# Down weights of the expert loop loaded through ScalarE's DMA queue, up weights through SyncE's

## What is computed

```python
def moe(h, w_router, b_router, w_gu, b_gu, w_down, b_down):
    logits = (xt @ w_router + b_router).astype(jnp.float32)
    top_v, top_i = lax.top_k(logits, TOP_K)          # 4 of 32 experts per token
    gates = jax.nn.softmax(top_v, axis=-1)
    ...
    gu = xblk @ w_gu[e] + b_gu[e]                    # 1024 x 2048 per expert
    gate = jnp.minimum(gu[:, :D_EXPERT], SWIGLU_LIMIT)
    up = jnp.clip(gu[:, D_EXPERT:], -SWIGLU_LIMIT, SWIGLU_LIMIT)
    act = (up + 1.0) * (gate * jax.nn.sigmoid(SWIGLU_ALPHA * gate))
    return act @ w_down[e] + b_down[e]               # 1024 x 1024 per expert
```

## Time and profile before

| | us |
|---|---|
| median of 3 runs | 1126.22 (1125.59 to 1127.43) |
| the profiled execution, its time | 1125.18 |
| its span in the profile | 1123.40 |
| PE busy | 1091.3 (97% of the span) |
| VectorE busy | 246.7 (22%) |
| ACT busy | 108.8 (10%) |
| GpSimd (POOL) busy | 28.7 (3%) |
| HBM read | 433.66 MB, 387 GB/s over the span |

### The profile page before, as it was taken

The page is one execution under the profiler, slowest core; times in us unless marked ns, Lnnn a source line. Parts: engine busy times, 40 slices in busy tenths (PEclk is TensorE's granted clock), DMA queues, the critical chain, the costliest instruction groups (busy, mean ns, idle before and its releaser), DMA issues.

```text
span 1123.4 us, 12562 instructions
## 1 busy us (share of the span) xinstructions
PE 1091.3 (97%) x5328; PEld 486.5 (43%) x5329; DVE 246.7 (22%) x580; ACT 108.8 (10%) x245; POOL 28.7 (3%) x43
## 2 busy tenths in 40 slices
PE   8999999999999999999999999999999999999996
PEld 6758887734333333333333333333333333333322
DVE  3263212332121212121212221111121212121121
ACT  1152120300000000000000000000000000000001
POOL 1240000000000000000000000000000000000000
PEclk9999999999999999999999999999999999999998
DMA  9964386489999999999999999999999999999996
GB/s 355 407 239 167 113 294 244 184 348 422 418 419 438 431 433 431 429 429 431 433 436 431 434 431 429 429 431 435 435 431 433 431 429 429 432 426 428 423 420 258
DMA packets 31149, 435.14 MB, mean 387 GB/s; under 512 B 4560, under 2 KB 5328, under 8 KB 8720
## 3 DMA queue, kind: packets, MB, share of 16 engines
q1 hardware_dynamic: 30272, 432.76, 91.7%
q10 hardware_dynamic: 848, 1.97, 0.5%
HBM read 433.66 MB, written 1.05 MB: 387 GB/s over the span
## 4 chain that ended last, share of the span: by engine, by line
PE 65%; DMA 32%; DVE 2%; issue 0%; ACT 0%; SPq 0%; POOL 0%; ACTq 0%; DVEq 0%
DMA ring<-in_up 29%; PE ps L1595 26%; PE ps L1613 11%; PE ps L1396 5%; PE ps L1621 3%; PE ps L1494 3%; PE ps L1410 2%; PE ps L1279 2%; DMA ring<-in_last_down 2%; PE ps L1604 2%; PE ps L1472 2%; PE ps L1340 1%; PE ps L1579 1%; DMA ring<-in_front 1%; PE ps L1478 1%; PE ps L1573 1%
## 5 line engine op out<-in xcount | busy, mean ns | idle before, releaser
L1595 PE MATMUL ps<-ring,work 128*64 128x512 f32 x2044 | 471.2, 606 | 17.9 <-DMA ring<-in_up 17.8
L1595 PEld LDWEIGHTS ps<-ring,work 128*64 128x64 f32 x2044 | 141.1, 138 | 313.8 <-issue 278.0
L1613 PE MATMUL ps<-ring,work 128*64 128x512 f32 x992 | 220.3, 596 | 1.3 <-DMA ring<-in_down 1.3
L1076 DVE TENSOR_SCALAR work<-ps 128x512 f32<-128x512 f32 x32 | 22.1, 692 | 624.9 <-PE ps L1595 624.9
L1613 PEld LDWEIGHTS ps<-ring,work 128*64 128x64 f32 x992 | 68.3, 137 | 130.4 <-issue 122.8
L1494 PEld LDWEIGHTS ps<-work 128*128 128x128 f32 x512 | 62.1, 191 | 23.5 <-issue 22.8
L1494 PE MATMUL ps<-work 128*128 128x128 f32 x512 | 70.5, 282 | 0.5 <-DVE work L1019 0.5
L1621 PE MATMUL ps<-work 64*128 64x512 f32 x256 | 63.6, 615 | 0.1
L1396 PE MATMUL ps<-work,ring 128*128 128x256 f32 x256 | 56.6, 379 | 0.0
L1396 PEld LDWEIGHTS ps<-work,ring 128*128 128x128 f32 x256 | 48.6, 190 | 6.5
L716 ACT ACTIVATE work<-ps 128x256 f32<-128x256 f32 x33 | 12.6, 383 | 356.1 <-PE ps L1579 356.1
(11 more groups left out here) (190 smaller groups left out, 549.8 us busy)
## 6 DMA issues: line engine op xcount, KB each, us to landing
ring<-in_up SPq DMA_DIRECT2D x48, 4096.0 KB, 42.8
ring<-in_down SPq DMA_DIRECT2D x24, 4096.0 KB, 41.8
ring<-in_up SPq DMA_DIRECT2D x46, 1024.0 KB, 10.0
ring<-in_front SPq DMA_DIRECT2D x22, 1024.0 KB, 13.5
ring<-in_down SPq DMA_DIRECT2D x20, 1024.0 KB, 9.7
ring<-in_up SPq DMA_DIRECT2D x8, 2048.0 KB, 49.5
ring<-in_down SPq DMA_DIRECT2D x4, 2048.0 KB, 47.0
ring<-in_last_down SPq DMA_DIRECT2D x3, 1024.0 KB, 26.7
```

The lines of the kernel that those rows point to most:

```text
L1076: return dve.tensor_scalar(up_c, ps[:, UP, :], LIMIT, -LIMIT, ALU.min, ALU.max)
L1595: last = pe.matmul(ps[n * CAP:(n + 1) * CAP, bank, :], x, w[bank - GATE][:, n * BANK:(n + 1) * BANK], start=k == 0, stop=k == KT - 1, skip ...
L1613: done = pe.matmul(ps[n * CAP:(n + 1) * CAP, bank, :], act_of(k), w[:, n * BANK:(n + 1) * BANK], start=first, stop=last, skip_group_check= ...
```

## The change

In turns 2 to 13 the groups 2 and 5 (down weights) are no longer issued by SP but by ACT, right behind the copy of `y_e` of the expert that used these slots in the turn before. SP's loop keeps the four groups of up weights. The loads have the same sizes, sources, destinations and semaphores. To leave out turns 14 and 15, ACT's loop runs one round less and that round is written out. Turns 0, 1, 14 and 15 are loaded as before. `unit` moves out of SP's program so that both use it.

```diff
+        def unit(i, g):
+
+            u, j = divmod(g, PER_EXPERT // SPAN)
+            if j < UP_SLOTS // SPAN:
+                return up_rows[:, bass.ds(i * (PAIR * UP_SLOTS // SPAN) + (u * UP_SLOTS // SPAN + j), 1), :]
+            return down_rows[:, bass.ds(i * (PAIR * DOWN_SLOTS // SPAN) + (u * DOWN_SLOTS // SPAN + j - UP_SLOTS // SPAN), 1), :]
...
@@ block.sync
-            def unit(i, g):
...
             with sp.Fori(2, TURNS - 2) as i:
                 for g in range(RING // SPAN):
-                    group_load(i, g)
+                    if g % (PER_EXPERT // SPAN) < UP_SLOTS // SPAN:
+                        group_load(i, g)
...
@@ block.scalar
                     act.wait_ge(freed, i * (UNROLL * PER_EXPERT) + (N_FRONT + (u + 1) * PER_EXPERT))
                     act.activation(y_e, ps[:, Y, :], ACT.Copy).then_inc(y_ready, 1)
+                    turn = i * (UNROLL // PAIR) + u // PAIR
+                    if not isinstance(i, int) or 0 < turn < TURNS - 3:
+                        g = (u % PAIR + 1) * (PER_EXPERT // SPAN) - 1
+                        act.dma_start(ring[:, SPAN * g:SPAN * (g + 1), :], unit(turn + 1, g)).then_inc(grouped[g], 16)
 
             first_pair()
             experts(0)
-            with act.Fori(1, E // UNROLL - 1) as i:
+            with act.Fori(1, E // UNROLL - 2) as i:
                 experts(i)
+            experts(E // UNROLL - 2)
             experts(E // UNROLL - 1)
             last_pair()
```

## The result

| | before | changed |
|---|---|---|
| median | 1126.08 us (1125.25 to 1127.43, 13 runs) | 1129.70 us (1127.86 to 1132.94, 13 runs) |
| the profiled execution | 1125.18 us, span 1123.4 | 1132.93 us, span 1131.1 |

The ratio is 1.0035, 95% interval 1.0026 to 1.0044: slower by 3.6 us, clear of noise. The forecast was 1133.4 us. The runs fall on two levels: nine at 1127.9 to 1130.0 us, four at 1132.1 to 1132.9. The profiled execution is one of the upper four, so its +7.7 us is more than the median shows.

The account below looks back on a forecast made before the run. PE was taken as the bound until about 690 us, then the DMA engines (58.28 us a turn). Later up weights gave +8.3 or +6.0 us; the middle, +7.2 us on 1126.2, made 1133.4 us, range 1125.5 to 1138.5.

Parts of the forecast that it names:

- Step 1: Issuing 24 down loads on ACT instead of SP, 0.33 us each, costs nothing: ACT idles about 10 us there.
- Step 2: Down loads in their own queue share the engines equally, packet by packet, landing 19.4 us after issue instead of 46 to 48.
- step 3: Each expert's second up group lands 11.9 us later plus half of PE's wait; some 2 us pass until a transfer flows.
- Rival A: Engines alternate between the two queues by whole loads, not packets: +5.1 us, median 1131.3 us; chance 0.20.
- Steps 3 and 4: Up weights land 11.9 us later plus half the wait; PE first waits 4.4 us near 555 us, then 3.04 us per turn.
- Step 5: Loss falls at turn 13's second up group, landing at 966.7 us; later loads land as before; end 1131.7 us, +8.3 us.
- the 5.0 us of waits that vanish: PE's waits for weights from 953.38 us to the end (3.1 + 1.3 + 0.6), forecast to disappear, leaving 165.0 of 170.0 us.
- Step 6: Last wait may instead be the second expert's second up group in turn 12, 937.6 us: +6.0 against +8.3 us; middle +7.2.
- B: No change, 1126.2 us: engines serve requests in issue order whatever the queue, or PE's delay is absorbed; chance 0.12.
- C: Faster: two queues fill gaps between loads, needing 437 GB/s or more; at 2% the median is 1120.1 us; chance 0.04.
- D: ACT's queue gets under the third of engine time down loads need; PE waits for down weights; about 1149 us; chance 0.07.

Follow-up runs that it names:

- the second profile: The changed kernel run once more without an edit: median 1129.65 us, ratio 1.0035; its profiled execution took 1129.74 us, span 1127.9 us.

## Why the prediction was right, and where it was off

- **Step 1, issue.** Right. 0.34 us on ACT, and the kernels with 20 and 22 loads through ACT are level with the kernel before.
- **Step 2, order and sharing.** Right: packet for packet, shown by 118 of 121 steps that change the queue. A load lands after 23.5 us, not 19.4, nor 21.4 with the 2 us of step 3. Rival A, whole loads in turn, falls by the same steps. The forecast took it for the rule of the Trainium skill ("DMA: Bandwidth & Descriptors", "Queues, rings and completion order") that an engine drains a whole packet of typically 9 to 17 descriptors from a queue before it switches. Here the unit of alternation is the packet as the profile counts it, one of 32 KB; how many of the page's descriptors such a packet holds no run shows, so what falls is the forecast's reading of the rule as a whole load. The other rule, of the Trainium skill ("DMA: Bandwidth & Descriptors", "Issuing engines are not separate DMA queues"), that loads issued from several engines run on the same 16 DMA engines and gain only issue time, agrees: 432 GB/s before and after.
- **Steps 3 and 4, the lateness and the first wait.** Right in size and place (559.08 for about 555, 3.39 for 4.4 us; G1 of turn 13 lands 13.7 us later than before, 967.07 against 953.33, for 13.4). "Once per turn, 3.04 us" was too regular: waits of 1.6 to 4.2 us came 29 to 87 us apart, depending on whether the clock had fallen before.
- **Step 5, where it is lost.** The mechanism is right: G1 of turn 13 was forecast for 966.7 and began at 967.11 and 966.91, the loads behind it land when they did (the first of the last weights at 1104.04 us, before 1103.65), and the removal of one turn from the set took the loss away. The mis-sized term is the 5.0 us of waits that vanish. Without slow clocks the stretch from that point is 168.3 us before (170.0 less 1.70) and 161.0 after: 7.3 us of waiting were in it. The rows of idle time give 5.0 in eleven waits. Where the rest is can be read by laying the timelines of PE before and of the second profile beside each other: the distance between equal rows shrinks from 11.79 to 4.55 us, and only at the waits. At G4 of turn 13, for one, it shrinks by 0.67 us where the idle row says 0.44, and one wait of 0.19 us has no idle row at all (48 matmuls in 10.66 instead of 10.47 us, at 1057.66). So a wait hides between 0.07 and 0.27 us. That it is the modelled end of the pipelined matmul ahead, from which idle time is counted, is likely but not shown.
- **Step 6, the two phases.** Both exist. The upper was forecast at +8.3 and has +7.7 in the profiled pair; the lower at +6.0 and has +4.5 in the second profile (1127.9 against 1123.4). I took the middle; 15 of 22 runs lie on the lower level, so the median is nearer to it. That, some 2.2 us of hidden waits, and some faster runs on the lower level (down to 1127.9 us, without a profile, so their cause is open) make 3.6 us out of the 7.2 forecast. The forecast missed the size by a factor of two, and only the range held it.
- **Rivals.** B (nothing changes) falls by the interval; C by 432 GB/s; D did not occur, and its price was about right when an edit brought it about.

## What to carry to other kernels

Where DMA is the bound, as here, a second queue added no bandwidth (432 GB/s with one or two); it changed the order in which bytes arrive, and the single queue that is issued in the order of use is the one to keep. Bytes that come before they are needed are paid for by those that come after, and the bill is the lateness at the last reordered load less what the rest of the kernel can catch up: compute the time at the last place where the order differs, not per iteration. A change of order can be free in the middle of a stream and cost most when it touches its end.

## What the runs showed of the hardware beyond what was expected

- The share of a queue follows its packet size: at 32, 16 and 8 KB beside SP's 32 KB ACT's queue had 3.96 beside 4.75 MB (20 us of the loop, ACT's queue being empty for part of it), 1.69 beside 3.44 MB, and 0.97 beside 4.19 MB (12 us each), which is too little to keep up. Cutting a load into smaller ones demotes its queue.
- The same wait does or does not bring the clock down: after 2.14 to 2.15 us of idling 16 matmuls took 3.65 us (848.63) or 5.35 us (877.76) in one execution; after some 4 us, in the changed kernel's profile, they took 5.30 to 6.60 us. So the place of the waits in a stream that DMA bounds differs from run to run, and at its end 3 us of time with it.
- A small share of one kernel's time can hang on such a state: the change has runs 5.1 us apart, the kernel before 2.2. One profiled execution would have doubled the loss.
